# Attention by pairs of heads, with the division by the sums on GpSimd

## The chip, the cores and the metric

The kernel runs on one core of one Trainium2 chip. The metric is device time in microseconds (us) of one launch. Five queues of instructions run side by side and wait for each other through semaphores: TensorE (PE; its weight loads are listed as PEld), VectorE (DVE), ScalarE (ACT), GpSimd (POOL) and SyncE (SP), which here only issues transfers. TensorE reads from SBUF and writes to PSUM (eight banks of 512 float32 per partition); GpSimd works in SBUF alone in this kernel.

## The reference

256 tokens of width 1024, float32. Two blocks of the first kind, then two of the second, then a last norm.

```python
# first kind, twice
proj = rms_norm(x) @ w_in                       # q, k, v of 8 "na" heads; q of 8 "gqa" heads, their 2 k, 2 v
na  = softmax(q @ k.T / 8 + bias) @ v           # 8 heads of width 64, 256 keys, masked by the bias
gqa = softmax(rope(norm(q)) @ rope(norm(k)).T / 8) @ v      # 8 heads of width 64, 256 keys
x = x + concat(na, gqa) @ w_out
x = x + (softmax(q @ mem_k.T / sqrt(128)) @ mem_v) @ w_mem_o   # "mem": 4 heads of width 128, 256 keys
x = x + conv_ffn(rms_norm(x))                   # up, a convolution of 3 taps, silu(gate) * val, down
# second kind, twice
x = x + 0.5 * swiglu(rms_norm(x))
h = rms_norm(x)
dil = softmax(q @ k.T / 8 + log_count) @ v      # 16 heads of width 64, causal: 128 keys, then 256
ssd = mamba2(silu(conv4(xbc)), dt, z)           # xbc: 16 tiles of 128 features, a convolution of 4 taps
x = x + concat(ssd, dil) @ w_out_2
x = x + 0.5 * swiglu(rms_norm(x))
```

## The kernel before

All weights pass once through SBUF, in 608 halves of 128x1024 float32, in the order in which they are used. A half is loaded into `RAW` (5 slots), ScalarE rounds it into `WH` (`highs`, 4 slots), VectorE subtracts to get the rest, `WL` (`lows`, 4 slots). Each product of a weight with activations is three TensorE products in the rounded type: high by high, low by high, high by low. So each half costs ScalarE one ACTIVATE, VectorE one TENSOR_TENSOR and TensorE 24 products of 256 columns (or 12 of 512). ScalarE and VectorE go through the same list of steps as TensorE and stay up to three halves ahead (`AHEAD`).

The three big programs (`pe_program`, `act_program`, `dve_program`) are written by hand, each in its own order. What is written after something in a program stands behind it on that engine, whatever it waits for. Every helper records on one line: L83 a product, L86 a transposition on TensorE, L92 a copy with scale on ScalarE, L94 and L95 other ScalarE functions (L95 those with a sum), L98, L104, L105, L108 VectorE's elementwise forms, L111 a copy (VectorE or GpSimd), L114 a maximum, L117 a reciprocal.

Attention (four kinds: na, gqa, mem, dil) does one head at a time. For head i:

- TensorE: scores, 128 queries by 128 or 256 keys, twice. They are float32 products, and the profile shows each as two passes. The contraction is over the head's width, so a head of 64 uses partitions 0 to 63 or 64 to 127 of q and k ("64*128"). All scores go to bank 4 (`SCB`).
- VectorE: scale and bias, maximum. ScalarE: exponentials with their sums. VectorE: reciprocal. ScalarE: multiplication by it (`exp_t(j)` onto itself).
- TensorE: 3 or 4 transpositions into bank 5 (`TRB`). ScalarE copies them out to `prob_t`. TensorE: values, 64 columns of v as weights ("128*64"), to partitions 0 to 63 or 64 to 127 of bank 6 (`OB`). ScalarE and VectorE take the high and low part of the result of a pair.

Within the loop, `fill.beat()` runs steps of other work between the parts of a head: TensorE's step is a tile of some projection, and the other two engines run their part of the same step. The steps use banks 0 to 3 (`WT`), the sums use bank 7 (`STB`). na has the gqa projections, the gqa values and the first of the four memory key tiles as steps; gqa has the rest of these tiles and the first half of the output projection; mem has the memory values; dil has half of its own values and 16 tiles of `xbc`. An `xbc` step is: TensorE one tile, ScalarE a copy and the first tap (with the bias), VectorE three more taps, ScalarE a tanh, VectorE `xc_end` (tanh plus one times the sum).

In TensorE's loop iteration i the order is: scores of head i, steps, values of head i-2, transpositions of head i-1.

GpSimd only spreads the key scales over 64 columns (`widen`, 36 copies), SyncE issues the transfers.

## Time and profile before

| | |
|---|---|
| time, median of 3 runs | 2207.64 us (2207.12 to 2211.21) |
| the profiled execution | 2210.88 us, of which 2209.0 us are the span of the trace |
| PE busy | 2093.2 us (95%) |
| DVE busy | 1344.9 us (61%) |
| ACT busy | 1153.6 us (52%) |
| POOL busy | 15.4 us (1%) |
| granted TensorE clock, mean | 0.98 of full |

Stretches of the attentions in the trace: na 55.1 to 118.1 and 464.1 to 524.4, gqa 118.1 to 157.0 and 524.4 to 563.3, mem 185.1 to 210.5 and 591.4 to 616.8, dil 1093.8 to 1212.1 and 1777.2 to 1895.5. Together they are 489 of the 2209 us. TensorE is the engine to look at: it is busy nearly everywhere, and where it sits idle in front of a group the row says so in brackets, with the engine whose result came last. Matmuls are pipelined, so the mean duration of one (0.4 us for a pass of 256 columns) is longer than the time from one start to the next.

### The profile page before, as it was taken

How to read it: one execution, taken by the hardware profiler on the slowest of the kernel's cores; microseconds unless marked ns; L12 is line 12 of the kernel's file. 1: busy time of each engine (PE TensorE's matmuls, PEld its weight loads, DVE VectorE, ACT ScalarE, POOL GpSimd, SP SyncE). 2: the span in 40 equal slices, each digit the busy share in tenths (PEclk: the TensorE clock that was granted, in tenths of full speed). 3: DMA queues.
4: the chain of work that ended last, by engine and by line, in shares of the span. 5: the costliest groups of instructions: out<-in, count | busy, mean ns of one | idle time of the engine just before them, and what ended most of it. 6: DMA issues, size and time to landing. Idle time of an engine off the chain costs nothing.

```text
span 2209.0 us, 30726 instructions
## 1 busy us (share of the span) xinstructions
PE 2093.2 (95%) x12212; PEld 1797.1 (81%) x12212; DVE 1344.9 (61%) x2344; ACT 1153.6 (52%) x2024; POOL 15.4 (1%) x40
## 2 busy tenths in 40 slices
PE   7999799999989999999988889999999999889999
PEld 6768799887879987888977768888888977758887
DVE  5655687555568856555566666555555566757554
ACT  5666465456556644445566435444444556535443
POOL 0000000000000000000100000000000010000000
PEclk9999999999999999999999999999999998989999
DMA  7223356542325655555422335555555432315554
GB/s 280 66 96 127 101 194 226 173 134 78 131 89 173 194 192 177 183 187 173 144 86 86 106 99 185 184 183 187 184 181 190 153 102 80 124 58 167 184 182 134
DMA packets 90111, 329.93 MB, mean 149 GB/s; under 512 B 9968, under 2 KB 10352, under 8 KB 89584
## 3 DMA queue, kind: packets, MB, share of 16 engines
q1 hardware_dynamic: 89968, 327.97, 45.0%
q8 instruction: 97, 1.59, 0.3%
q14 instruction: 46, 0.38, 0.1%
HBM read 326.88 MB, written 1.05 MB: 148 GB/s over the span
## 4 chain that ended last, share of the span: by engine, by line
PE 77%; DVE 12%; ACT 7%; issue 4%; DMA 0%; POOL 0%; SPq 0%; DVEq 0%; ACTq 0%
PE PS L83 74%; DVE TMP L108 3%; ACT WH L92 3%; PE PS L86 3%; DVE WL L98 3%; ACT TMP L95 1%; ACT TMP L94 1%; DVE SM L114 1%; DVE TMP L98 1%; DVE TMP L105 1%; DVE GL L108 1%; DVE SM L108 1%; ACT TMP L92 0%; ACT GH L92 0%; DVE M L108 0%
## 5 line engine op out<-in xcount | busy, mean ns | idle before, releaser
L98 DVE TENSOR_TENSOR WL<-RAW,WH 128x1024 fp32r<-128x1024 f32 x608 | 741.9, 1225 | 624.9 <-ACT WH L92 620.4
L92 ACT ACTIVATE WH<-RAW 128x1024 fp32r<-128x1024 f32 x608 | 640.8, 1056 | 485.9 <-PE PS L83 479.2
L83 PE MATMUL PS<-WH,GH 128*128 128x512 f32 (+2 forms) x944 | 370.8, 393 | 2.2 <-DVE WL L98 2.2
L83 PE MATMUL PS<-WL,GH 128*128 128x512 f32 (+2 forms) x944 | 362.8, 384 | 0.0
L83 PE MATMUL PS<-WH,GL 128*128 128x512 f32 (+2 forms) x944 | 362.5, 384 | 0.0
L83 PE MATMUL PS<-GH,WH 128*128 128x256 f32 x1096 | 321.2, 293 | 14.4 <-DVE WL L98 9.3
L83 PE MATMUL PS<-GL,WH 128*128 128x256 f32 x1096 | 315.3, 288 | 0.0
L83 PE MATMUL PS<-GH,WL 128*128 128x256 f32 x1096 | 315.1, 287 | 0.0
L83 PE MATMUL PS<-WH,HH 128*128 128x512 f32 (+2 forms) x768 | 286.1, 373 | 0.0
L83 PE MATMUL PS<-WH,HL 128*128 128x512 f32 (+2 forms) x768 | 283.5, 369 | 0.0
L83 PE MATMUL PS<-WL,HH 128*128 128x512 f32 (+2 forms) x768 | 283.5, 369 | 0.0
L83 PEld LDWEIGHTS PS<-GH,WH 128*128 128x128 f32 x1096 | 214.5, 196 | 23.7 <-issue 9.6
L83 PEld LDWEIGHTS PS<-WH,GH 128*128 128x128 f32 x944 | 179.6, 190 | 43.2 <-issue 8.7
L83 PEld LDWEIGHTS PS<-GL,WH 128*128 128x128 f32 x1096 | 214.7, 196 | 0.0
L83 PEld LDWEIGHTS PS<-GH,WL 128*128 128x128 f32 x1096 | 214.6, 196 | 0.0
L83 PEld LDWEIGHTS PS<-WH,GL 128*128 128x128 f32 x944 | 179.5, 190 | 35.2
L83 PEld LDWEIGHTS PS<-WL,GH 128*128 128x128 f32 x944 | 179.8, 190 | 31.6
L83 PE MATMUL PS<-HH,WH 128*128 128x256 f32 x584 | 175.6, 301 | 21.4 <-DVE HL L108 8.5
L83 PE MATMUL PS<-HL,WH 128*128 128x256 f32 x584 | 170.3, 292 | 0.0
L83 PE MATMUL PS<-HH,WL 128*128 128x256 f32 x584 | 169.9, 291 | 0.0
L83 PEld LDWEIGHTS PS<-WH,HH 128*128 128x128 f32 x768 | 144.8, 189 | 25.5 <-issue 1.7
L83 PEld LDWEIGHTS PS<-WH,HL 128*128 128x128 f32 x768 | 144.8, 188 | 24.4
(136 smaller groups left out, 2428.7 us busy)
## 6 DMA issues: line engine op xcount, KB each, us to landing
RAW<-wts SPq DMA_DIRECT2D x608, 512.0 KB, 4.0
M<-bias SPq DMA_DIRECT2D x2, 2048.0 KB, 13.2
X<-x SPq DMA_DIRECT2D x2, 512.0 KB, 5.8
TMP<-mem SPq DMA_DIRECT2D x1, 1024.0 KB, 12.2
out<-X SPq DMA_DIRECT2D x4, 256.0 KB, 3.3
CST<-cst SPq DMA_DIRECT2D x1, 706.0 KB, 9.9
M<-gf SPq DMA_DIRECT2D x1, 512.0 KB, 4.7
PAR<-par SPq DMA_DIRECT2D x1, 368.0 KB, 7.1
```

The lines of the kernel that those rows point to most:

```text
L83: return Issued(self.eng and self.eng.matmul(o, l, r, start=first, stop=last, skip_group_check=share))
L86: return Issued(self.eng and self.eng.transpose(o, i, ident))
L92: return Issued(self.eng.activation(o, i, f, scale=scale))
L94: return Issued(self.eng.activation(o, i, f, bias=bias, scale=scale))
L95: return Issued(self.eng.activation(o, i, f, bias=bias, scale=scale, accum_out=acc))
L98: return Issued(self.eng and self.eng.tensor_tensor(o, a, b, op))
L105: return Issued(self.eng.tensor_scalar(o, a, s1, s2, o0, o1))
L108: return Issued(self.eng and self.eng.scalar_tensor_tensor(out=o, in0=a, scalar=s, in1=b, op0=o0, op1=o1))
L114: return Issued(self.eng and self.eng.tensor_reduce(o, i, AX.X, ALU.max, negate=True))
```

## The change

1. Attention works on pairs of heads. `scores(i)` puts the scores of heads 2i and 2i+1 next to each other, to two banks (3 and 4), alternating between the heads, which stand on different partitions; `weigh(i)` does the same with the values. The transpositions stay by head (`turn_probs`), in one bank. The steps between are given by tables of rates.
2. The division by the sums moves from ScalarE to GpSimd (`divide`, two TENSOR_SCALAR for each head, on `exp_t(j)` onto itself), with a semaphore of its own (`scaled`).
3. `WT` shrinks from four banks to three. `prob_t` gets a second buffer.
4. The values and the last two key tiles of na become steps inside na, 8 of them in its first iteration. The memory gains (`memory(k)`) are spread over na's steps. Two of the memory key tiles stand between na and gqa.
5. The memory values are one product of 512 columns instead of two of 256.
6. In dil, the second half of the values and all key scales stand ahead of the attention. In an `xbc` step the copy out of PSUM is gone: VectorE's taps read PSUM themselves, and the tanh goes to `XC`, with `band_t` (6 buffers) as the sum.

```diff
-        WT, SCB, TRB, OB, STB = (0, 1, 2, 3), (4,), (5,), (6,), (7,)
+        WT, SCB, TRB, OB, STB = (0, 1, 2), (3, 4), (5,), (6,), (7,)
...
         def prob_t(i):
-            return TMP[:, 2560:3072]
+            return TMP[:, 2560 + i % 2 * 512:3072 + i % 2 * 512]
...
+        NA_RATES = [3, 3, 2] + [0.67] * 12
+        GQA_RATES = [0.67] * 15
+        MEM_RATES = [2, 2, 2, 1, 1, 0, 1, 1, 2]
+        DIL_RATES = [0.6] * 27
...
# pe_program, new; in turn_probs the wait is now for `scaled`
+                def scores(i):
+                    ps = []
+                    for j in (2 * i, 2 * i + 1):
+                        ps.append(take((a, "s", j), SCB[j % 2:j % 2 + 1]))
...
+                    for t in range(2):
+                        for u in range(2):
+                            h = heads[2 * i + u]
+                            m = e.mm(ps[u][:, keys_of(widths, t)], h["q"][t], h["k"][t], True, True)
...
+                for i in range(n + 1):
+                    if i < n:
+                        scores(i)
+                    for u in range(2):
+                        if i >= 1:
+                            turn_probs(2 * i - 2 + u)
+                        fill.beat(next(rate))
+                    if i >= 1:
+                        weigh(i - 1)
+                    fill.beat(next(rate))
...
# act_program, the loop, new
+                for i in range(n + 1):
+                    for u in range(2):
+                        if i >= 1:
+                            probs(2 * i - 2 + u)
+                        if i < n:
+                            exps(2 * i + u)
+                        fill.beat(next(rate))
+                    fill.beat(next(rate))
+                    if i >= 1:
+                        high(i - 1)
...
# dve_program, the loop, new
+                    if i < n:
+                        maxima(2 * i)
+                        maxima(2 * i + 1)
+                    if i >= 2:
+                        low(i - 2)
+                    fill.beat(next(rate))
+                    for u in range(2):
+                        if i < n:
+                            inverse(2 * i + u)
+                        fill.beat(next(rate))
...
# pool_program
+            def divide(a, n, widths):
+                for j in range(n):
+                    den = smc(522 + 4 * (j % 4), 2)
+                    e.wait_ge(small, (a, "den", j))
+                    for t in range(2):
+                        sl = keys_of(widths, t)
+                        m = e.ts(exp_t(j)[:, sl], exp_t(j)[:, sl], den[:, t:t + 1], None, ALU.mult)
+                    m.then_inc(scaled, (a, "p", j))
...
# act_program, an xbc step
-                        e.act(ACT.Copy, u[:, 0:S], bank(key)[:, 0:S]).then_inc(ready, ("u0", L, m))
-                        e.act(ACT.Identity, u[:, 260:516], bank(key)[:, 0:S], scale=col(w + 48),
...
+                        highs(("xbc", L, m))
+                        yield
+                        band(m)
+                        if m >= 1:
+                            tanh(m - 1)
```

How this moves instructions, on three places. First TensorE at the beginning of na in the first block (`M` holds q, k and v, `TMP` the probabilities, `CST` the identity). Before, the scores of heads 0 and 1 follow on the values, and one tile (24 products) stands ahead of the first transpositions:

```order
242 L83 MATMUL PS<-WH,HH 128x512
243 L83 MATMUL PS<-WL,HH 128x512
244 L83 MATMUL PS<-WH,HL 128x512
245 L83 MATMUL PS<-M 128x256 x4
246 L83 MATMUL PS<-HH,WH 128x256
...
270 L86 MATMUL PS<-CST,TMP 128x128 x4
271 L83 MATMUL PS<-M 128x256 x2
```

After, 48 products of 512 columns (the values) stand between the first scores and the first transpositions:

```order
149 L83 MATMUL PS<-M 128x256 x4
150 L83 MATMUL PS<-WH,HH 128x512
...
197 L83 MATMUL PS<-WH,HL 128x512
198 L83 MATMUL PS<-M 128x256 x4
199 L86 MATMUL PS<-CST,TMP 128x128 x8
200 L83 MATMUL PS<-HH,WH 128x256
```

So the steps moved ahead of the point where TensorE first needs probabilities; and the transpositions of two heads (x8) now stand together.

Second, TensorE in the middle of gqa. Before, one head: scores, a step of six products, values, transpositions:

```order
570 L83 MATMUL PS<-M 128x256 x2
571 L83 MATMUL PS<-WH,GH 128x512
...
576 L83 MATMUL PS<-WH,GL 128x512
577 L83 MATMUL PS<-TMP,M 64x256 x2
578 L86 MATMUL PS<-CST,TMP 128x128 x4
```

After, two heads:

```order
548 L83 MATMUL PS<-M 128x256 x4
549 L86 MATMUL PS<-CST,TMP 128x128 x8
550 L83 MATMUL PS<-WH,GH 128x512
...
555 L83 MATMUL PS<-WH,GL 128x512
556 L83 MATMUL PS<-TMP,M 64x256 x4
557 L83 MATMUL PS<-WH,GH 128x512
```

The scores and values of a pair are adjacent, and so are its transpositions, with no step between the first four and the second four.

Third, ScalarE in the middle of dil. Before, one head: copy of the transposed, the two divisions (L92 `TMP<-TMP,SM`), the exponentials (L95), the half, and the copy and first tap of the `xbc` tile:

```order
711 L92 ACTIVATE TMP<-PS 128x384
712 L92 ACTIVATE TMP<-TMP,SM 128x128
713 L92 ACTIVATE TMP<-TMP,SM 128x256
714 L95 ACTIVATE TMP,SM<-TMP,SM 128x128
715 L95 ACTIVATE TMP,SM<-TMP,SM 128x256
716 L92 ACTIVATE WH<-RAW 128x1024
717 L92 ACTIVATE TMP<-PS 128x256
718 L94 ACTIVATE TMP<-PS,PAR 128x256
719 L94 ACTIVATE TMP<-TMP 128x256
```

After:

```order
669 L92 ACTIVATE TMP<-PS 128x384
670 L95 ACTIVATE TMP,SM<-TMP,SM 128x128
671 L95 ACTIVATE TMP,SM<-TMP,SM 128x256
672 L94 ACTIVATE TMP<-PS,PAR 128x256
673 L94 ACTIVATE M<-TMP 128x256
674 L92 ACTIVATE WH<-RAW 128x1024
675 L92 ACTIVATE TMP<-PS 128x384
```

Three of nine are gone, and the first tap and the tanh, of an earlier tile than before, now stand ahead of the half's ACTIVATE.

## Rows read from the trace of the kernel before

**Rows 1.** Page, parts 1 and 4: busy time, and the chain that ended last.
```profile
PE 2093.2 (95%) x12212; PEld 1797.1 (81%) x12212; DVE 1344.9 (61%) x2344; ACT 1153.6 (52%) x2024; POOL 15.4 (1%) x40
...
PE 77%; DVE 12%; ACT 7%; issue 4%; DMA 0%; POOL 0%; SPq 0%; DVEq 0%; ACTq 0%
```
**Rows 2.** Busy time by stretch: na, gqa, na, dil, dil, and na's beginning.
```profile
core 0: us, PE busy (x) PEld busy (x) DVE busy (x) ACT busy (x) POOL busy (x), PEclk, DMA share, GB/s
55.10:118.10 63.00, 59.92 (x370) 48.85 (x370) 38.09 (x88) 37.03 (x88) 0.52 (x2) 0.92 0.24 75
118.10:157.00 38.90, 37.19 (x170) 23.73 (x169) 18.26 (x46) 26.57 (x65) 0.00 (x0) 1.00 0.25 82
464.10:524.40 60.30, 57.21 (x372) 46.57 (x371) 37.69 (x88) 39.13 (x91) 0.53 (x2) 0.97 0.25 81
1093.80:1212.10 118.30, 104.79 (x665) 85.48 (x664) 76.10 (x188) 72.78 (x187) 3.28 (x9) 0.96 0.27 86
1777.20:1895.50 118.30, 108.41 (x664) 89.15 (x664) 76.12 (x188) 72.76 (x187) 3.22 (x9) 0.93 0.27 86
...
56.50:63.30 6.80, 6.05 (x23) 5.21 (x24) 3.35 (x8) 4.04 (x11) 0.00 (x0) 0.50 0.02 8
```
**Rows 3.** PE in time, first scores of na: start, length, [idle before].
```profile
55.09 1.13 PE L83 MATMUL PS<-M 64*128 64x256 f32 x4 [1.05 <-ACT M L92]
57.25 2.07 PE L83 MATMUL PS<-M 64*128 64x256 f32 x4 [1.03 <-DVE TMP L108]
```
**Rows 4.** PE in time, gqa: a head in the middle, and the end.
```profile
146.01 1.08 PE L83 MATMUL PS<-TMP,M 128*64 128x256 f32 x4
147.02 0.66 PE L86 MATMUL PS<-CST,TMP 128*128 128x128 f32 x4
147.61 1.13 PE L83 MATMUL PS<-M 64*128 64x256 f32 x4
148.67 0.50 PE L83 MATMUL PS<-WH,GH 128*128 128x512 f32 x1
...
155.97 1.08 PE L83 MATMUL PS<-TMP,M 128*64 128x256 f32 x4 [0.75 <-ACT TMP L92]
```
**Rows 5.** PE group by shape, whole trace: busy us, mean ns | idle before.
```profile
L83 PE MATMUL PS<-TMP,M 128*64 128x256 f32 x256 | 77.5, 405 | 31.2 <-ACT TMP L92 15.9 <-DVE GL L98 9.2 <-DVE M L108 6.1
```
**Rows 6.** PE in time, dil: the values of two heads that follow each other.
```profile
1177.12 0.85 PE L83 MATMUL PS<-TMP,M 128*64 128x256 f32 x4 [0.67 <-DVE GL L98]
...
1183.95 0.86 PE L83 MATMUL PS<-TMP,M 128*64 128x256 f32 x4 [1.48 <-ACT TMP L92]
```
**Rows 7.** Waits in dil (1093.8 to 1212.1): us in total, times, longest.
```profile
DVE WL L98 <- ACT WH L92: 32.2, 18, 2.0
ACT TMP L94 <- DVE TMP L108: 28.0, 13, 3.9
```
**Rows 8.** ACT groups by shape in dil, same stretch.
```profile
L92 ACT ACTIVATE TMP<-TMP,SM 128x256 f32<-128x256 f32 x16 | 7.9, 494 | 0.0
L92 ACT ACTIVATE TMP<-TMP,SM 128x128 f32<-128x128 f32 x16 | 6.4, 398 | 5.5 <-DVE SM L117 5.5
L92 ACT ACTIVATE TMP<-PS 128x256 f32<-128x256 f32 x15 | 5.5, 363 | 2.0 <-PE PS L83 2.0
```
**Rows 9.** GpSimd's copies in time, at three places.
```profile
106.23 0.52 POOL L111 COPY SQ<-SM 128x128 f32<-128x128 f32 x2 [105.79 <-DVE SM L117]
...
1089.96 2.35 POOL L111 COPY SQ<-SM 128x128 f32<-128x128 f32 x1 [576.92 <-DVE SM L104]
...
1098.23 1.52 POOL L111 COPY SQ<-SM 128x128 f32<-128x128 f32 x2 [3.73 <-PE PS L83]
```
**Rows 10.** DVE in time beside the last two of these.
```profile
1089.81 2.36 DVE L98 TENSOR_TENSOR WL<-RAW,WH 128x1024 fp32r<-128x1024 f32 x2
...
1098.26 1.33 DVE L98 TENSOR_TENSOR WL<-RAW,WH 128x1024 fp32r<-128x1024 f32 x1 [2.00 <-ACT WH L92]
```
**Rows 11.** PE in time, na: the transposition behind the memory gains.
```profile
107.23 0.73 PE L86 MATMUL PS<-CST,TMP 128*128 128x128 f32 x4 [2.04 <-ACT TMP L92]
```

More of the change, by code:

```diff
@@ L573, in block1 @@
                 rms_over(("mix", L))
-                for m in range(1, 4):
-                    fm_tile(("nk", L, m), mix)
+                fm_tile(("nk", L, 1), mix)
                 if L == 0:
@@ L631, in values @@
                 def values():
-                    for b in range(2):
-                        tm_tile(("mv", L, b), mkv, 256, WT)
-                        yield
-                    yield
-                    yield
+                    yield from tm_wide(("mv", L), mkv, 512, WT)
                     acts = [(GH[:, m, :], GL[:, m, :], (("mem", L), m)) for m in range(2)]
                     yield from residual(("mo1", L), acts, allowed=WT)
-                fill = Steps(values(), 1.0)
-                attention(("mem", L), mem_heads(L), [256, 256], fill, two=False)
+                fill = Steps(values())
+                attention(("mem", L), mem_heads(L), [256, 256], fill, MEM_RATES, two=False)
                 fill.rest()
@@ L1539, in rope_scales, with rope_all, memory, memory_key @@
                             small, ("scq", L))
-                def rest():
+                def rope_all(m):
+                    rope(m)
+                    rope_end(m)
+                def memory(k):
+                    e.wait_ge(ahi, (("mkv", L), k))
+                    e.stt(Lw(1 - side, k), MEMX[:, k, :], col(pb + P_MKV + k), H(1 - side, k).bitcast(F32),
+                          ALU.mult, ALU.subtract).then_inc(alo, (("mkv", L), k))
+                def memory_key(m):
+                    key = ("mk", L, m)
+                    e.wait_ge(tile, key)
+                    e.copy(MK[:, m, :], bank(key)[:, 0:S]).then_inc(dout, key)
@@ new lines, in block1, with onward @@
+                rope_all(4)
+                rope_scales()
+                lows(("mk", L, 0))
+                lows(("mk", L, 1))
+                memory_key(0)
+                e.wait_ge(spread, ("gk", L))
+                e.wait_ge(made, ("gq", L, 4))
+                e.tt(GK, GK, bank(("gk", L))[:, 0:S], ALU.mult).then_inc(dout, ("gk", L))
+                def onward():
+                    for m in range(2, 4):
+                        lows(("mk", L, m))
+                        memory_key(m - 1)
+                        yield
+                    memory_key(3)
@@ L1590, in values @@
                 def values():
-                    for b in range(2):
-                        lows(("mv", L, b))
+                    for i in range(KD):
+                        lows((("mv", L), i))
                         yield
-                    yield
-                    yield
                     yield from residual(("mo1", L), 2)
-                fill = Steps(values(), 1.0)
-                attention(("mem", L), mem_heads(L), [256, 256], fill, two=False)
+                fill = Steps(values())
+                attention(("mem", L), mem_heads(L), [256, 256], fill, MEM_RATES, two=False)
                 fill.rest()
```

534 lines of the change are left out of this document (263 added, 271 removed).

## The prediction

> **What bounds the kernel now.** I read the page first, then the busy time by stretch, then TensorE in order of time inside each attention. TensorE is busy 95% of the span and carries 77% of the chain that ended last [rows 1]: time is won only by giving it fewer or shorter passes, or by taking away what it waits for. The reader should then look at the stretches of the attentions [rows 2]. In dil TensorE is idle 13.5 us (118.3 less 104.79) and 9.9 us (118.3 less 108.41). In na it is idle 3.1 us in each block, in gqa 1.7. Idle is not all: the granted clock is 0.96 and 0.93 in dil, 0.92 in the first na. A stretch at 1.2 GHz among 2.4 GHz makes that mean: 8% and 14% of the two dils are at the low level, some 26 us together, which cost half of themselves, 13 us. The last row of [rows 2] is such a stretch, 6.8 us, right behind the two waits with which na begins [rows 3].
>
> Two more things don't show as idle. First, passes of heads of width 64 use half of the array's rows (scores) or columns (values). Four passes of 256 columns last 1.08 us with one at 0.405 us, so they start (1.08 - 0.405) / 3 = 0.22 us apart [rows 4, 5]. Second, going to another kind of product costs: from the values to the transpositions 1.01 us pass, from the scores to the next product 1.06 [rows 4], where four starts of 0.22 make 0.88, so 0.13 to 0.18 us each time.
>
> In dil's middle the values of one head follow those of the last by 6.83 us (1177.12 to 1183.95) [rows 6]. Of that 1.48 are the idle right in front of the values, so some 5.3 are passes. The waits say why: VectorE's subtraction waits for ScalarE's half 18 times, 32.2 us, and ScalarE's tanh waits for VectorE's taps 13 times, 28.0 us [rows 7]. Each stands in the other's way once a head. Neither is full: VectorE 76.1 and ScalarE 72.8 us busy of 118.3 [rows 2].
>
> **The change part by part**, against the profiled execution of 2210.88 us (span 2209.0). It lies 3.2 us above the median of 2207.64; I take the differences over to the median.
>
> *Pairs side by side.* Two heads' scores are on different partitions of the inputs and go to different banks; their values go to different partitions of one bank. Nothing in this trace has such passes next to each other in steady state, so the price lies between nothing and all. If they can overlap, and if passes start in the order written, the two passes of one head still follow each other; the second of one runs with the first of the other. Eight passes then take the time of five: 3 x 0.22 = 0.66 us saved for scores and as much for values. na and gqa have 16 pairs (two blocks of eight): 16 x 1.32 = 21 us. In dil half of the passes have 128 columns; of the three that are saved two are half as long: 0.44 us, twice, for 16 pairs: 14 us. Together 35. mem's heads use the whole array and gain nothing. In dil other engines are near and will take part of it back. I take two thirds, 23 us; the ends are 0 and 35.
>
> This row-less term is where the Trainium skill bears most. TensorEngine Tiling (Array Packing), Key Properties, says that tiles of the array work independently and that a change of the tiling mode drains the engine. The second half agrees with the 0.13 to 0.18 us above; the first no row here shows. By that page's factor of up to two for a contraction of at most 64 the term would be 49 us as an estimate (four passes saved of eight instead of three).
>
> *Fewer switches, new hand-overs.* By head there were switches into scores, values and transpositions, about 0.5 us; by pair now the same, so 36 pairs save some 18 us. Against it: all eight transpositions of a pair go through one bank. Where no step stands between the two fours, TensorE waits until ScalarE has copied the first out. The end of gqa shows this hand-over bare: transpositions, a wait of 0.75 us, values [rows 4]; the bracket counts from the modelled end of the last pass, and from where the next could have started I put it at 0.9. By the tables the rate 0.67 gives steps in the pattern none, one, one, so it happens in each of the 16 iterations of na and gqa behind the first; dil's 0.6 makes it 4 times in both blocks together, and 8 times no step stands between the second four and the values. 28 x 0.9 = 25 us. Net +7; if the other engines are late at these points it is up to +25, if the copies are hidden -18.
>
> *dil's waits.* ScalarE loses, per head, two divisions (494 and 398 ns) and a copy (363 ns) [rows 8]: 1.26 of some 4.5 us. The tanh no longer waits for taps of the step just begun, and the half is rounded ahead. VectorE keeps its work. Without four subtractions and six key scales, which now stand ahead, it has about 76.1 - 4.9 - 2.5 = 69 us for 16 heads, 4.3 us a head, against 5.3 of TensorE. So TensorE is next, with VectorE close behind. What there is to get is 23.4 us idle and 13 of clock. Late next are VectorE's two maxima in a row and the locks told below. I take 26 us; ends 0 and 36.
>
> *na's beginning.* 48 products of the values, 11 us, now cover the first softmax. Gone are the waits of 1.05 and 1.03 us [rows 3] and most of 6.8 us at half clock [rows 2], 3.4 us: 5.5. The second block's na lasts 2.7 us less, so 2.8 are left to get there. Together 8.3; ends 4 and 12. The work itself moves without a price: products, roundings and subtractions are the same.
>
> *The memory gains.* Eight ScalarE and eight VectorE operations stood in one step and held the transpositions up for 2.04 us [rows 11], in each block. Spread, they hold nothing. But the gqa key scale is now wanted one tile (3 us) after the last rotation, and the chain to it (three VectorE operations, a Newton iteration, GpSimd's copies) is some 5 us. Net -2 us; ends -4 and +4.
>
> *Three banks instead of four.* In mem and in the SSD part that follows dil, the second half of a projection needs two banks while the first half's two are not both read. TensorE waits for one addition on VectorE, about 1 us, in four places: +4; ends 0 and 8. The joined memory values I count as nothing (0 to 3 saved).
>
> *The division on GpSimd.* It is hidden if it ends before the transpositions want it. They want it an iteration later, 8 us or more behind the scores; maximum, exponential and reciprocal take about half of that. A copy of 128 columns lasts 0.26 to 0.3 us (two in 0.52) [rows 9]; two of 256 columns then some 1.2. Cost nothing, if this holds.
>
> Here a second rule speaks, and against the change. First the rows: a copy that takes 0.26 us took 2.35 beside two subtractions of 2.36, and both ended together; another pair took 1.52, and the subtraction beside it 1.33 instead of 1.22 [rows 9, 10]. The Trainium skill, SBUF — State Buffer, Who interferes with whom, says that a VectorE instruction with two inputs in SBUF and a GpSimd instruction that reads SBUF shut each other out for their whole length. By that rule, the trace agrees. Each division can be held for 1.2 us and more, and each can hold VectorE by its own length. I count it inside dil's term.
>
> Sum: -23 + 7 - 26 - 8.3 - 2 + 4 = -48.3 us. 2207.6 - 48.3 = 2159.
>
> **The rivals.**
> *The pairs don't overlap.* For it: the trace has no case, and the passes are of float32, two for each product. Against it: different rows, different banks. The time is 2159 + 23 = 2182.
> *dil stays where it is*, since VectorE takes the place of the old cycle: maxima of two heads in a row, then a subtraction that waits for ScalarE, plus divisions that hold it. For it: VectorE's 4.3 us a head lie only 1.0 below TensorE's, and less if the pairs overlap. Against it: ScalarE is a quarter freer. The time is 2159 + 26 = 2185.
> *The hand-overs don't appear* and the pairs overlap in full: 2159 - 25 - 12 = 2122; half of it is as likely, 2135.
> *GpSimd becomes the wait (the slower side).* Place: the transpositions, which wait for `scaled`. If each division lasts as long as the held copy, 2.35 us, a pair takes 9.4 us, more than a pair's time in gqa (4 x 2.1 us at most) and about dil's; TensorE then waits some 2 us a pair, 36 x 2 = 72 us: 2159 + 72 = 2231. It decides from 48 / 36 = 1.3 us a pair on. For it: [rows 9, 10]. Against it: the long copies ran into two subtractions back to back, and in attention the subtractions stand alone, one for each head.
>
> **How the numbers follow.** Forecast 0.45, no overlap 0.2, dil unchanged 0.1, the better case 0.13, GpSimd 0.09, a mixture near no change 0.03. The range takes the forecast's own (2140 to 2178), both milder rivals and half of the better case, with the ends of the unknown terms: 2118 to 2203. A difference of 0.2% (4.4 us) is what a measurement of this kernel tells from none. Faster 0.88, the same 0.03, slower 0.09.
>
> **What would show it.** Pairs: in gqa the eight passes of a pair's scores within 1.4 us instead of 1.9 from first start to next group. Hand-overs: an idle of 0.7 us or so in front of every second group of transpositions in na and gqa, by ScalarE's copy. dil: both stretches, with the values ahead of them counted, near 105 us, and both waits of [rows 7] under 10 us. Beginning of na: no wait in front of the first transpositions and no stretch at half clock. GpSimd: divisions near 0.5 us each, idle before the next. I am wrong in kind if PE waits at transpositions for GpSimd by more than 20 us in all, and wrong in size if scores and values of a pair start no closer than 0.22 us.

## The result, and the profile after

| | median of the runs, us | profiled run, us | span, us | mean granted clock |
|---|---|---|---|---|
| before | 2209.43 (2207.12 to 2212.84) | 2210.88 | 2209.0 | 0.980 |
| changed | 2174.52 (2172.88 to 2175.91) | 2173.6 | 2171.7 | 0.979 |

The ratio is 0.9841, with a 95% interval from 0.9823 to 0.9858: 35 us faster, where 48 were forecast (2159). The sign and the range were right. The sum was near partly by luck: two of its terms were off by 20 us and more, in opposite directions, as the terms show further down. (The 2209.43 us are the median of four runs; the forecast started from the 2207.64 us of the first three.)

The page of the changed kernel, part 1, against [rows 1]:

```profile
PE 2023.6 (93%) x12116; PEld 1760.0 (81%) x12116; DVE 1343.9 (62%) x2344; ACT 1082.6 (50%) x1848; POOL 155.9 (7%) x184
```

TensorE is busy 69.6 us less and the span is only 37.3 us shorter, so idle time has grown by 32 us. Where, busy time by stretch tells: first the kernel before, cut at the end of gqa, behind the first half of the memory's output projection (`mo1`), the same in the second block, the start of dil with its key scales, its end, and so on; then the changed kernel, cut at the same points, with dil's values (ahead of its attention now) counted in dil.

```profile
4.60:157.00 152.40, 138.03 (x815) 110.87 (x815) 85.66 (x195) 93.10 (x203) 0.52 (x2) 0.97 0.42 148
157.00:213.50 56.50, 52.72 (x330) 47.06 (x330) 31.44 (x65) 33.98 (x69) 0.00 (x0) 0.97 0.37 122
213.50:563.30 349.80, 332.00 (x2180) 292.29 (x2178) 234.46 (x434) 201.50 (x369) 0.53 (x2) 0.99 0.45 149
...
1092.60:1212.10 119.50, 105.99 (x672) 86.52 (x672) 76.52 (x189) 73.96 (x188) 4.48 (x14) 0.96 0.27 88
1212.10:1776.00 563.90, 548.87 (x2921) 466.72 (x2920) 324.48 (x466) 263.99 (x377) 2.64 (x3) 0.99 0.50 165
...
```

```profile
4.70:148.20 143.50, 118.58 (x815) 100.45 (x815) 85.12 (x195) 78.06 (x172) 36.21 (x34) 0.99 0.44 154
148.20:205.30 57.10, 51.85 (x282) 44.84 (x281) 33.30 (x67) 30.33 (x60) 8.95 (x8) 0.97 0.41 133
205.30:547.70 342.40, 316.17 (x2180) 285.29 (x2178) 232.76 (x433) 186.15 (x338) 37.07 (x34) 0.98 0.46 151
...
1077.10:1187.10 110.00, 91.96 (x674) 80.15 (x673) 77.63 (x192) 59.46 (x145) 30.47 (x48) 0.94 0.31 101
1187.10:1750.00 562.90, 547.82 (x2921) 466.01 (x2920) 322.68 (x463) 262.46 (x373) 2.80 (x4) 0.99 0.50 164
...
```

The two parts with na and gqa gained 8.9 and 7.4 us. The stretch with the memory attention lost 0.6 us in each block (56.5 to 57.1). The two dils gained 9.5 and 9.8 us (the second 119.5 to 109.7). What the change leaves alone moved little: 472.8 to 472.3 ahead of dil, 563.9 to 562.9 between the dils, 310.0 to 308.4 behind. A cut has to fall on the same product in both kernels. Here both do 12 products of the output projection, 3.0 us, between the last memory values and the cut; with the cut right at the last values in one kernel alone, 3.6 us would seem lost in place of 0.6. The counts tell whether cuts agree: 2180 products lie in the next stretch of both.

TensorE's idle time (length less busy time) grew by 10.6 and 8.4 us in the parts with na and gqa, by 1.5 in each memory stretch and by 4.5 and 8.0 in the dils. In the first dil TensorE is idle 18.0 us of 110.0 where it was idle 13.5 of 119.5: dil got shorter because its passes did, and not because it waits less.

TensorE in order of time shows why the passes did (gqa, second block: start, length, form, count, idle before):

```profile
524.26 1.08 PE L83 MATMUL PS<-TMP,M 128*64 128x256 f32 x8
525.28 0.50 PE L83 MATMUL PS<-WH,GH 128*128 128x512 f32 x1
...
526.86 1.13 PE L83 MATMUL PS<-M 64*128 64x256 f32 x8
527.92 0.66 PE L86 MATMUL PS<-CST,TMP 128*128 128x128 f32 x4
529.27 0.66 PE L86 MATMUL PS<-CST,TMP 128*128 128x128 f32 x4 [0.69 <-ACT TMP L92]
529.68 0.49 PE L83 MATMUL PS<-WH,GH 128*128 128x512 f32 x1
```

Eight passes of a pair take what four of one head took in [rows 4]: 1.06 us for the scores (526.86 to 527.92) and 1.02 for the values. They have the time of four, not of five. And the hand-over is there as forecast: 1.35 us from the first group of transpositions to the second, 0.41 from the second to what follows, so 0.94 lost, with the idle 0.69 by ScalarE's copy. This stands at 12 of the 16 pairs of na and gqa. At the other four, the first and the last pair of each gqa, the second group waits longer, 1.35 and 1.88 us, for its division on GpSimd:

```profile
522.31 0.63 PE L86 MATMUL PS<-CST,TMP 128*128 128x128 f32 x4 [1.35 <-POOL TMP L104]
```

### The profile page after: what moved, and what is told of

It reads as the page before. It is cut to its first block, busy times and chain, and to the rows that moved or that the text cites. A ratio compares the mean times of both kernels' runs of the same rounds, so it can differ in the third digit from the quotient of the medians.

```text
span 2171.7 us, 30543 instructions
## 1 busy us (share of the span) xinstructions
PE 2023.6 (93%) x12116; PEld 1760.0 (81%) x12116; DVE 1343.9 (62%) x2344; ACT 1082.6 (50%) x1848; POOL 155.9 (7%) x184
## 4 chain that ended last, share of the span: by engine, by line
PE 78%; DVE 9%; ACT 7%; issue 3%; POOL 1%; POOLq 0%; DVEq 0%; ACTq 0%
PE PS L83 75%; PE PS L86 3%; DVE TMP L108 3%; ACT WH L92 3%; DVE WL L98 2%; ACT TMP L95 2%; ACT TMP L94 1%; DVE TMP L98 1%; DVE SM L114 1%; DVE TMP L105 1%; ACT TMP L92 1%; POOL TMP L104 1%; DVE GL L108 0%; DVE SM L108 0%; ACT M L92 0%
## 5 line engine op out<-in xcount | busy, mean ns | idle before, releaser
L92 ACT ACTIVATE WH<-RAW 128x1024 fp32r<-128x1024 f32 x608 | 641.2, 1057 | 498.0 <-PE PS L83 491.1
L104 POOL TENSOR_SCALAR TMP<-TMP,SM 128x256 f32<-128x256 f32 (+1 forms) x144 | 137.3, 966 | 604.8 <-DVE SM L117 593.2
```

Source lines behind the costliest of these rows:

```text
L92: return Issued(self.eng.activation(o, i, f, scale=scale))
L104: return Issued(self.eng.tensor_scalar(o, a, s1, None, o0))
```

## The experiments

All are edits of the changed kernel, so its ratio of 0.984 (0.982 to 0.986) is what each is held against; 0.001 is 2.2 us, and differences in us from the changed kernel's time are taken from the ratios. What is said of single stretches is read from one profiled execution of each kernel. Executions of one kernel differ too: the four of run 5's first kernel took 2170.07 us (mean clock 0.982) to 2177.61 us (0.975). For the comparisons, the changed kernel's first gqa, second na, first dil without its values, and what stands between the dils up to the second one's attention:

```profile
112.70:148.20 35.50, 30.90 (x194) 22.41 (x193) 19.42 (x48) 20.34 (x50) 15.46 (x16) 1.00 0.23 75
439.50:499.30 59.80, 54.82 (x391) 46.41 (x391) 36.66 (x69) 33.31 (x78) 19.03 (x16) 1.00 0.35 115
1092.50:1187.10 94.60, 77.08 (x593) 67.58 (x594) 70.00 (x180) 52.84 (x137) 25.63 (x32) 0.93 0.27 87
1187.10:1765.30 578.20, 562.71 (x3001) 478.68 (x3000) 329.99 (x474) 267.91 (x379) 6.17 (x16) 0.99 0.50 164
```

**1. The order of a pair's passes.** For scores (values alike):

```
-                    for t in range(2):
-                        for u in range(2):
+                    for u in range(2):
+                        for t in range(2):
```

> The changed kernel with the same two heads beside each other, but all passes of the one head's scores ahead of all of the other's, and the values likewise; the number of instructions, of hand-overs and the fill are the same. Theory A, passes run together only with a direct neighbour that has the other 64 rows (scores) or the other 64 columns (values): of three places where one product meets the next, one is left, so a pair's scores in gqa take about 1.6 us instead of 1.06 and its values about 1.5 instead of 1.01; 16 pairs of na and gqa by 1.0 us and 16 of dil by 0.7 us are 28 us, and the time is 2195 to 2205. Theory B, what was saved is the switch to a new kind of product and the row halves have no part in it: 1.06 and 1.01 us stay, and the time is 2174 (2171 to 2178).

2174.04 us, ratio 0.983 (0.982 to 0.985): no change, and the time of the pair's scores is the same.

```profile
129.34 1.14 PE L83 MATMUL PS<-M 64*128 64x256 f32 x8
```

Theory A, neighbours only, is wrong. The starts of single passes in this trace say more. The first head's last pass, the one that signals its scores, is the fourth in the order written; it starts as the seventh, at 130.090 us, 13 ns ahead of the second head's last, and so all four passes of the one head start beside those of the other. But B's second half (the rows have no part in it) wasn't shown by this run, so the next one asked for that.

**2. Both heads on the same 64 rows.**

```
-                            h = heads[2 * i + u]
+                            h = heads[2 * i]
                             m = e.mm(ps[u][:, keys_of(widths, t)], h["q"][t], h["k"][t], True, True)
```

> Changes what is computed: the second head of each pair multiplies the first head's queries and keys again, so that both products of a pair lie on the same 64 rows of TensorE; number, shapes, banks and hand-overs stay. The four matmuls of a pair's scores took 1.06 us in na and gqa and about 0.86 us in dil, as long as the two of one head did before the change, even with one head's ahead of the other's. Theory A, the row halves work for themselves and each takes its own passes in order: on one half the pair takes twice as long, 16 pairs by 0.85 to 1.06 us and 16 pairs by 0.64 to 0.8 us, 24 to 30 us in all less what dil's waits hide: 2190 to 2205, and starts 0.21 us apart each. Theory B, what was saved is the gap where one shape follows another, and the rows have no part in it: no change, 2171 to 2178, and 1.06 us stay.

2190.15 us, ratio 0.992 (0.990 to 0.994): 17 us slower. (What it computes isn't the reference's.)

```profile
527.72 1.99 PE L83 MATMUL PS<-M 64*128 64x256 f32 x8
529.64 0.66 PE L86 MATMUL PS<-CST,TMP 128*128 128x128 f32 x4
```

1.92 us from start to next group instead of 1.06. The time is what theory A says, at the lower end of its range, and its sum is less (17 for 24 to 30): a part of it hides in waits (the first dil lasts 2.0 us more, with 14.7 us of idle time instead of 17.5). Together with run 1: the two halves of the rows each work through their own passes in order, and don't wait for each other, even when all of one head's passes are written ahead of the other's. The Trainium skill, TensorEngine Tiling (Array Packing), Key Properties, says that different tiles can execute in parallel; the runs agree. Both heads' values on the same 64 columns were not tried; that the columns behave like the rows is read from 1.02 us for eight passes alone.

**3. The hand-over, by moving the fill.**

```
-        NA_RATES = [3, 3, 2] + [0.67] * 12
-        GQA_RATES = [0.67] * 15
+        NA_RATES = [3, 3, 2] + [1, 1, 0] * 4
+        GQA_RATES = [1, 1, 0] * 5
```

> The changed kernel with another table of rates for na and gqa: of three places in a step for the fill, the first two (behind each head's transpositions) get one step of fill each and the third none, so that a step of projections stands between the two heads' transpositions and between them and the values, as it did before the change. The fill is as long (two steps for three places). Theory A, the hand-over of the one transposing bank costs 0.93 us wherever two heads' transpositions meet, 16 times: 15 us faster than the changed kernel, 2158 to 2163. Theory B, the wait moves to the values, whose operands come from ScalarE behind the second head's copy, or to the scores, which now follow the values directly: 2170 to 2176. A time above 2180 would mean that the fill was better where it was.

2170.96 us, ratio 0.982 (0.980 to 0.983): inside theory B's range, at its lower end. The stretches of the run tell more than the sum (second block's na and gqa; first dil with its values; what follows it):

```profile
435.40:491.80 56.40, 53.93 (x390) 46.34 (x390) 36.83 (x69) 33.72 (x77) 17.70 (x16) 1.00 0.38 121
504.90:538.20 33.30, 30.31 (x194) 22.46 (x193) 18.63 (x46) 20.12 (x49) 15.01 (x16) 1.00 0.25 81
...
1064.90:1177.50 112.60, 93.06 (x674) 81.07 (x674) 78.28 (x194) 59.41 (x145) 30.53 (x48) 0.92 0.31 99
1177.50:1743.90 566.40, 551.61 (x2922) 469.03 (x2920) 322.17 (x462) 262.46 (x373) 2.80 (x4) 0.98 0.50 163
```

Against 59.8 and 35.5 us in the changed kernel (both its gqas last 35.5), theory A holds where the edit is: 3.4 and 2.2 us. All that precedes dil is 12.2 us shorter (1077.1 to 1064.9). But dil lasts 2.6 us longer (110.0 to 112.6; clock 0.92 instead of 0.94), the code between the dils 3.5 (562.9 to 566.4; 0.98 instead of 0.99), the second dil 3.0, and the end 1.7. Nothing was edited there. Of these 10.8 us some 8 are TensorE's own products taking longer (551.6 us busy between the dils instead of 547.8, with no more idle time), which goes with the lower clock: the run's mean is 0.975 instead of 0.979. The other 3 are idle time in the two dils (19.5 us instead of 18.0 in the first). By the medians of four runs 3.6 us of the 12.2 are left.

**4. The hand-over, by banks.** Two runs: a bank taken from the fill, then one shared with the values.

```
-        WT, SCB, TRB, OB, STB = (0, 1, 2), (3, 4), (5,), (6,), (7,)
+        WT, SCB, TRB, OB, STB = (0, 1), (3, 4), (2, 5), (6,), (7,)
```

> Two PSUM banks for the transposed exponentials and two for the fill, instead of one and three; order and rates are those of the changed kernel. Theory A, the 0.7 us ahead of every second group of transpositions is the wait for the one bank's copy: it goes in na and gqa (16 times 0.93 us with what follows it) and at the few places of dil where two groups meet, and the fill waits for its banks by 0 to 6 us in all; 2158 to 2170. Theory B, the second group needs its exponentials only then: the idle time stays and gets another name, and the fill's third bank is missed, 2176 to 2190.

2209.58 us, ratio 0.9998 (0.999 to 1.001): the whole gain of the change is gone. na, first pair:

```profile
463.80 1.09 PE L86 MATMUL PS<-CST,TMP 128*128 128x128 f32 x8
468.75 0.58 PE L83 MATMUL PS<-GH,WH 128*128 128x256 f32 x1 [3.86 <-ACT M L92]
```

The eight transpositions now run in one go, so the 0.94 us was the wait for the one bank. But behind them the fill waits 3.9 us for a bank that ScalarE has yet to empty, and ScalarE empties it behind the softmax in its queue. Theory A had 0 to 6 us in all for the fill's waits and theory B ended at 2190 us; the measured time is outside both. In this na the two long waits are 3.9 us each, na lasts 67.7 us instead of 59.8 with a clock of 0.92 instead of 1.00, and gqa and dil last 3.8 and 4.3 us longer. Now shared with the values' bank:

```
+        WT, SCB, TRB, OB, STB = (0, 1, 2), (3, 4), (5, 6), (5, 6), (7,)
...
+                    if i >= 2:
+                        low(i - 2)
                     if i < n:
                         maxima(2 * i)
                         maxima(2 * i + 1)
-                    if i >= 2:
-                        low(i - 2)
```

> The transpositions and the values share two PSUM banks (before: one for each), and on VectorE the subtraction that frees the values' bank stands ahead of the next pair's maxima; the fill keeps its three banks. Within a pair the second group of transpositions then has a bank of its own, and the values take the first group's, whose copy they need anyway. Theory A, the idle 0.7 us at each second group is the wait for the one bank: it goes in na and gqa (16 times 0.93 us, as at the places where two banks for transpositions took it away) and at some places of dil, and the fill doesn't suffer: 2156 to 2164. Theory B, the wait passes on to the values, who need the second group's copy: in na and gqa a step of fill stands between, so only gqa's few bare places show it; and what is gained there is lost again further on to TensorE's lower clock, as where the steps of fill were moved: 2166 to 2175.

2174.56 us, ratio 0.983 (0.982 to 0.985), theory B. na got 1.5 us shorter (58.3), gqa 0.3, dil 2.7 longer (its clock is 0.88 instead of 0.93, its idle time the same). In gqa the second group, where it had waited for the bank, now waits for its division:

```profile
519.33 0.63 PE L86 MATMUL PS<-CST,TMP 128*128 128x128 f32 x4 [1.36 <-POOL TMP L104]
```

**5. The division.** Two runs: back on ScalarE (GpSimd's `divide` does nothing, ScalarE scales both heads of a pair at the head of a step), and no division at all, the transpositions waiting for the exponentials.

> The changed kernel with the division by the sums back on ScalarE (two operations a head, both heads of a pair at the head of the step that transposes them), GpSimd dividing nothing. Theory A, the move to GpSimd was worth something: ScalarE in dil gets 16 times about 0.9 us more beside 53 us of 95, na and gqa 8 times 1.0 each; the transpositions wait for ScalarE, which has both heads' divisions, the copies of the transposed groups and the exponentials in one queue: 0.3 to 0.8 us at 28 pairs, 8 to 22 us slower than the changed kernel, 2183 to 2197. Theory B, GpSimd's division is itself what dil waits for (62 us of VectorE's waits are put to it, and it is the slower engine, 0.92 us per 256 columns): the time falls by 3 to 12 us, 2162 to 2171.

2174.52 us, ratio 0.984 (0.982 to 0.985): no difference, which neither theory said.

> Leaves out the division of the exponentials by their sums (the output is not normalised); the transpositions wait for the exponentials instead. It prices GpSimd's division and the sums' way through VectorE together. Theory A, hidden as predicted: in na, gqa and the memory attention nothing, in dil the few waits at the transpositions (2 to 3 us at four or five places of each dil), so 2160 to 2172. Theory B, the division is hidden wholly: 2172 to 2176. Theory C, it is what bounds dil, whose VectorE shows 62 us of waits by it: dil falls from 95 to near 85 us, and the time to 2150 or less.

2178.34 us, ratio 0.985 (0.984 to 0.987), above all three theories. gqa lasts 33.7 us instead of 35.5, and dil doesn't get shorter:

```profile
510.10:543.80 33.70, 30.95 (x194) 22.40 (x194) 19.32 (x48) 20.30 (x50) 0.00 (x0) 1.00 0.25 79
1087.10:1183.50 96.40, 78.71 (x592) 69.52 (x593) 70.48 (x181) 52.63 (x137) 0.00 (x0) 0.89 0.27 85
```

The changed kernel's dil lasts 94.6 us, clock 0.93. So the 62 us that GpSimd waits in dil (rows below) are its rest, and theory C is wrong. In gqa all four second groups now wait the same 0.69 us for ScalarE's copy: the bank's wait stood beneath the longer waits for GpSimd. In dil TensorE's idle time stays (17.7 us, 17.5 with the division): its 9.5 us of waits for GpSimd at the transpositions are gone, and its waits for ScalarE's copy at the values grow from 5.8 to 14.5 us. The wait only moved. GpSimd was as good a place as ScalarE, no better.

**6. dil.** The changed kernel's waits in dil (1092.5 to 1187.1; us in total, times, longest), which answer to [rows 7], and VectorE and TensorE in time where TensorE waits longest:

```profile
POOL TMP L104 <- DVE SM L117: 62.3, 12, 9.8
ACT TMP L95 <- DVE SM L114: 19.8, 9, 4.9
DVE WL L98 <- ACT WH L92: 18.8, 15, 2.4
...
PE PS L86 <- POOL TMP L104: 9.5, 7, 3.0
ACT M L94 <- DVE TMP L108: 9.3, 8, 2.3
```

```profile
1108.48 1.77 DVE L108 SCALAR_TENSOR_TENSOR SM<-SM 128x32 f32<-128x32 f32 x8
...
1110.88 1.22 DVE L98 TENSOR_TENSOR WL<-RAW,WH 128x1024 fp32r<-128x1024 f32 x1
1112.01 1.51 DVE L108 SCALAR_TENSOR_TENSOR TMP<-PS,PAR,TMP 128x255 f32<-128x255 f32 x3
1113.44 0.15 DVE L117 RECIPROCAL SM<-SM 128x2 f32<-128x2 f32 x1
```

```profile
1115.34 0.87 PE L86 MATMUL PS<-CST,TMP 128*128 128x128 f32 x3 [3.01 <-POOL TMP L104]
```

```profile
1113.69 1.50 POOL L104 TENSOR_SCALAR TMP<-TMP,SM 128x128 f32<-128x128 f32 x2 [4.83 <-DVE SM L117]
```

The row names GpSimd, whose two operations fill 1.50 us of the 3.01. But GpSimd started as soon as it had the reciprocal of 1113.44, and that stood on VectorE behind the dt chain (some seventeen small operations in a row), a weight part and three taps. Behind the gap the clock is at 1.2 GHz for 10.2 us (1115.1 to 1125.3, granted 0.50). Three runs asked what this is worth. First the reciprocals one place of fill earlier:

```
+                    if i < n:
+                        inverse(2 * i)
                     fill.beat(next(rate))
-                    for u in range(2):
-                        if i < n:
-                            inverse(2 * i + u)
-                        fill.beat(next(rate))
+                    if i < n:
+                        inverse(2 * i + 1)
+                    fill.beat(next(rate))
+                    fill.beat(next(rate))
```

> On VectorE each pair's reciprocals of the sums are taken one place of fill earlier: the first head's directly behind the maxima, the second's behind one place of fill instead of two. Theory A, dil's late transpositions (2 to 3 us at four or five places of each dil) come from a reciprocal that stands behind a step of conv taps, weight parts or the dt chain: 3 to 8 us faster in all, 2166 to 2172. Theory B, they come from the load on VectorE itself, whose maxima for the next pair stand behind the same fill (the kernel without a division waited as long): now VectorE waits for the exponentials ahead of its fill, and the time is 2174 to 2182.

2174.79 us, ratio 0.984 (0.982 to 0.986): theory B. gqa gained 1.8 us a block, as without a division; dil lost 1.9 in each block, at a clock of 0.89. Then the dt chain in dil's last five steps (`if m >= 11:` ahead of `next(dts, None)` on all engines):

> In dil the dt part (on VectorE some seventeen small operations in a row, 3.8 us, ahead of a weight part and three conv taps) is run with the last five of the sixteen steps of fill instead of the first five, on all engines. Theory A, dil's longest gap (5.7 us around the second pair's second head, and the 10.2 us at the lower clock behind it) is this chain on VectorE standing ahead of that head's reciprocal and the next maxima: the gap shrinks to under 2 us, and with it or near it the clock stretch, 4 to 8 us a dil: 2160 to 2168. Theory B, each step of fill costs VectorE about as much wherever it stands, and the gap moves to where the chain now is, with its own clock stretch: 2171 to 2178.

2180.68 us, ratio 0.986 (0.985 to 0.988): theory B's side, and 3 us above its range. The dils last 97.1 and 95.0 us instead of 94.6 and 94.4; in the first the idle time fell from 17.5 to 16.7 us and the clock from 0.93 to 0.90. Last, one tap in three left out (`for d in (1, 3)`), which leaves out a part of the convolution:

> Leaves out one of the three conv taps of every tile in dil's fill (so the convolution isn't the reference's): 16 operations of VectorE, 0.515 us each from start to start, in each of the two dils, nothing of any other engine. Theory A, VectorE sets dil's pace: its step of fill costs it about 3.2 us where TensorE's costs 2.96, and the heads' maxima another 1.3 us each; 8.2 us less on it shorten each dil by 5 to 8 us and bring back some of the lower clock there: 2155 to 2164. Theory B, dil is a chain of hand-overs from engine to engine, whose waits don't depend on how full one of them is: 1 to 2 us for each dil, 2168 to 2173.

2173.5 us, ratio 0.983 (0.982 to 0.985). The dils:

```profile
1093.60:1186.10 92.50, 78.11 (x592) 68.53 (x593) 64.15 (x168) 52.71 (x137) 25.83 (x32) 0.91 0.27 88
1768.00:1856.90 88.90, 74.51 (x593) 65.51 (x593) 64.46 (x168) 53.40 (x138) 25.84 (x32) 0.96 0.29 94
```

2.1 and 5.5 us for 8.2 us of work taken off VectorE in each: the time is 0.5 us above theory B's range, the dils lie between the theories. TensorE's idle time is 14.4 us in both dils, where it was 17.5 in the changed kernel's: some 3 us of waits are gone in each. The difference between the two dils is the clock (0.91 and 0.96). The code behind the first dil then lasts 581.9 us, where the changed kernel needs 578.2. VectorE's load has a price in dil but isn't all of it.

**7. The values ahead of the first attention again** (`fill.beat(8)` ahead of it on three engines, and rates that begin with three zeros).

> The values' projection (eight steps) ahead of the first attention again instead of in its first step; the other seven steps of fill stay where the change put them. Theory A, as in the forecast: the first transpositions then wait for scores, maxima, exponentials and division with nothing to do, 3 to 5 us in each of two blocks, and the clock falls to its lower level behind that gap: 5 to 12 us slower than the changed kernel, 2180 to 2187. Theory B, what stands ahead of that wait, and not the wait, decides, and the clock is lost elsewhere instead: 2173 to 2178.

2189.13 us, ratio 0.991 (0.989 to 0.992): 15 us slower, more than theory A said. The second block's na:

```profile
461.08 2.08 PE L83 MATMUL PS<-M 64*128 64x256 f32 x8 [2.62 <-DVE TMP L108]
```

and the stretch behind it:

```profile
460.50:470.70 10.20, 8.29 (x36) 7.11 (x37) 4.83 (x13) 7.12 (x21) 5.46 (x6) 0.50 0.02 6
```

With two heads at a time TensorE waits 2.62 us for VectorE to have taken the scores of both out of their banks, where it had waited 1.03 in [rows 3]. The stretch at the low clock behind it is 10.2 us long in this block. Before the change the second block's na had none at this place; the 6.8 us of [rows 2] are the first block's, and there this run has about as much (57.5 to 64.3, granted 0.52).

**8. All that helped, together**: the rates of 3, the reciprocals of 6 in na, gqa and the memory attention alone, and the gqa key's spread behind both memory key tiles, with a third tile ahead of the attention.

> The changed kernel with four edits in na and gqa: the fill's steps between the two heads' transpositions and before the values (as tried alone: 2.2 us for each gqa, 3.3 for the second na), the reciprocals of gqa one place earlier (tried alone: 1.8 us for each gqa), and the gqa key's spread moved behind both memory key tiles instead of between them, with a third one ahead of the key's first use (TensorE waits 4.7 us for it and 1.5 us for its product in each block). Dil is left alone. Theory A, these sum up to 8 to 9 us a block, 16 to 18 us, of which up to 10 us are given back at the lower clock, as in the runs before: 2158 to 2168. Theory B, all of it is given back, the sum of TensorE's gaps and lower clock being what it is: 2170 to 2176. By my first theory of independent terms it would be 2157.

2170.22 us, ratio 0.982 (0.981 to 0.983), five runs from 2169.11 to 2170.61: the lower edge of theory B. TensorE's wait for the key's spread fell from 4.70 to 2.04 us (first the changed kernel, then this one):

```profile
507.20 0.99 PE L83 MATMUL PS<-CST,SQ 128*128 128x128 f32 x4 [4.70 <-POOL SQ L111]
```

```profile
496.63 1.21 PE L83 MATMUL PS<-CST,SQ 128*128 128x128 f32 x4 [2.04 <-POOL SQ L111]
```

and what lies between this kernel's dils:

```profile
1174.50:1756.20 581.70, 566.55 (x3004) 481.71 (x3002) 329.50 (x473) 268.11 (x379) 6.20 (x16) 0.98 0.50 163
```

dil begins 14.6 us earlier than in the changed kernel (1092.5 to 1077.9), the span ends 4.6 us earlier. The rest, where nothing was edited, gave 10 us back: dil 2.0 and 2.9, between them 3.5, the end the rest. The interval touches the changed kernel's, so whether it beats that one isn't settled; it beats the kernel before by 40 us.

## Why the prediction came out

The time fell inside the range, but not by the sum as it was written: pairs brought 20 us more than forecast, dil's waits 24 us less, and that these two nearly cancel is luck. Of the prediction's own signs, pairs (1.06 us, under the mark of 1.4) and na's beginning held. The hand-over's 0.7 us stands at 12 of the 16 places. The dils missed their mark, and so did the division's 0.5 us. One sign says "wrong in kind": TensorE waits at transpositions for GpSimd 18 times, 25.4 us in all, where the mark was 20 (whole trace):

```profile
PE PS L86 <- POOL TMP L104: 25.4, 18, 3.0
```

What this wait means is taken up under the division.

*Pairs side by side* (forecast -23, ends 0 and 35) and *fewer switches* (-18). Mis-sized. The step that failed is "the second of one runs with the first of the other, eight passes take the time of five"; runs 1 and 2 show that the order written has no part in it and eight take the time of four. In na and gqa a pair saves 2.06 us, switches included: twice 1.06 and 1.01 [rows 4] less 1.06 and 1.02. 16 pairs make 33 us. In dil a head's values took 0.89 us from start to next group (1177.12 [rows 6] to 1178.01) and its scores 0.85 (the two rows below), then the changed kernel's scores:

```profile
1178.49 0.92 PE L83 MATMUL PS<-M 64*128 64x128 f32 x4
1179.34 0.39 PE L83 MATMUL PS<-HH,WH 128*128 128x256 f32 x1
```

```profile
1107.73 0.93 PE L83 MATMUL PS<-M 64*128 64x128 f32 x8
```

Eight passes last as long as four did (0.93 and 0.92), so some 1.75 us are saved for each of 16 pairs, 28 us. 61 in place of 41. The estimate of 49 us that the prediction made from the Trainium skill, TensorEngine Tiling (Array Packing), Theoretical Speedup (a factor of up to two), gives 67 with the 18 for the switches, nearer than 41.

*New hand-overs* (+25). Right in na and gqa: 0.94 us at 16 places, 15 us, where 14 of the 25 were put (at four of them it shows by itself only in run 5's kernel without a division). The 11 for dil can't be told apart from its other waits.

*dil's waits* (-26). This is the step that failed in kind. The share that pairs have in dil, 28 us, is more than the two dils gained, 19.3. So its waits, new hand-overs among them, took some 9 us where they were to bring 15 (26 less 11). Of [rows 7] the subtraction's wait fell from 32.2 to 18.8 us and the tanh's from 28.0 to 9.3, the first well above the mark of 10 and the second just below it. The wait of ScalarE's exponentials for VectorE's maxima grew to 19.8 us, from 8.4 before (the row below, 1093.8 to 1212.1). The mark of 105 us for dil was missed with 110.0 and 109.7.

```profile
ACT TMP L95 <- DVE SM L114: 8.4, 16, 1.9
```

The rival "VectorE takes the place of the old cycle" had the mechanism: two heads' maxima and reciprocals in one queue with the fill. That its load alone isn't the bound (run 6, taps), nor one chain's place in it (dt part), nor the reciprocals' place, is shown; that it is the cycle of hand-overs between VectorE and ScalarE remains argued. A dil without fill, with another table of rates, or with the maxima on another engine wasn't tried.

*na's beginning* (-8.3). Right in kind: both waits and the stretch at half clock are gone (na's clock is 1.00). Its size can only be had as what is left of the 16.3 us that na and gqa gained (33 for pairs, less 15 for hand-overs, 5 for the key's spread and 4 for the divisions): some 7 us, with two new waits of TensorE in each na, 0.65 and 1.54 us, in it. Against the pair's own longer softmax it is worth 15 us (run 7), which the sum hadn't asked.

*Memory gains and gqa key scale* (-2, ends -4 and +4). The wait of 2.04 us [rows 11] is gone, but TensorE waits 4.70 us for the spread in each block: +5 us, outside the ends.

*Three banks* (+4), *joined memory values* (0). Too high: the memory attention's stretch lost 0.6 us twice, 1.2 us, and I didn't divide it between the two; between the dils, where the SSD part stands, nothing was lost. The new waits there are 2.6 us for ScalarE's copies (two in 148.2 to 205.3), not for VectorE's addition. That a third bank is worth much was shown the other way round: with two the kernel is 35 us slower.

*The division on GpSimd* (0). The mark of 20 us was passed with 25.4, so by its own sign the prediction was wrong in kind here: 9.5 us of them are in each dil, 3.2 in each gqa. But what TensorE waits for is VectorE's reciprocals behind their fill as much as the division: without a division the dils are no shorter, and each gqa is 1.8 us shorter, as it also is with the division kept and the reciprocals one place earlier (run 6). So the cost of the term is 1.8 us in each gqa. The size of the operation was wrong too. By form over the whole run, and in time (two of 256 columns; the same beside a subtraction):

```profile
L104 POOL TENSOR_SCALAR TMP<-TMP,SM 128x256 f32<-128x256 f32 x112 | 115.6, 1041 | 469.3 <-DVE SM L117 469.3
```

```profile
116.45 1.82 POOL L104 TENSOR_SCALAR TMP<-TMP,SM 128x256 f32<-128x256 f32 x2 [8.79 <-DVE SM L117]
119.95 2.71 POOL L104 TENSOR_SCALAR TMP<-TMP,SM 128x256 f32<-128x256 f32 x2 [1.68 <-DVE SM L117]
```

1.82 us a head, where 1.2 was estimated from copies. The rival in which GpSimd becomes the wait needed 2.35 us for each division; it got 1.04. Two of the rivals' sums were also off: half of the way to 2122 is 2140 and not 2135, and 9.4 us against 4 x 2.1 leave 1.0 us a pair and not 2.

Against the forecast, then: 20 us more from pairs and 3 more from the memory stretch; 24 less from dil's waits, 7 from the key's spread, 4 from the divisions, 1 from the hand-overs and 1 from na's beginning; and 3 us gained in stretches that the change leaves alone (0.5, 1.0 and 1.6), which no term had. That makes 11 us, by which the spans' difference, 37.3, falls short of 48.3. It has to come out, since na's beginning and dil's waits were had by subtraction.

## What to carry to other kernels

Products that use half of the array's rows or columns belong next to each other, the one on one half and the other on the other; in which order the passes of one pair are written doesn't matter. A softmax for two heads at a time doubles what stands between two waits on the other engines, so it needs a longer step of fill in front (here 15 us, run 7), and a bank taken from the fill has a price (here 35 us for the step from three to two). In this kernel, with TensorE 93% busy, a wait taken away in one place came back elsewhere, mostly as time at the lower clock: read the granted clock and the idle time of the stretches that you didn't edit, and in more than one execution, before you call an edit useless or good. And when you compare stretches of two kernels, count the products on both sides of each cut.

## What of the hardware was not expected

- Two passes on different halves of the rows start some 0.01 us apart (526.860 and 526.867 us in the changed kernel, 129.338 and 129.352 in run 1), two on the same half 0.22 (1.92 us for eight starts and the switch in run 2). They need not start in the order written: in run 1 the fourth starts as the seventh.
- The same instructions between the two dils took 578.2 us in the changed kernel and 581.6 to 581.9 in four of the edited ones (runs 3, 5 without a division, 6 with a tap less, 8), beside a granted clock of 0.99 and 0.98, though nothing was edited there. Why the clock was lower in these is not shown.
- GpSimd's multiplication by a column takes 0.91 us for 256 columns (half of 1.82) undisturbed and 1.04 on the mean. For 128 columns it takes 0.60 us at the least, over twice its copy of as many in [rows 9].
